# The rank scans of two query tiles cut into four parts, and the selection steps of tiles 2 and 4 spread over more heads

## What is computed

```python
idx_score = jnp.where(admissible[None], idx_score, NEG)
_, sel = lax.top_k(idx_score, topk)          # topk = 256; of equal scores the lower index wins
...
scores = jnp.einsum('bqhd,bqkd->bhqk', qb, k_sel) * scale
scores = scores - slopes[None, :, None, None] * dist[:, None]
p = jax.nn.softmax(scores, axis=-1)
```

## Time and profile before

| | |
|---|---|
| median of 3 runs | 551.23 us (550.86 to 551.24) |
| the profiled execution | 551.45 us |
| its span, first to last instruction | 549.6 us |
| PE busy | 541.5 us (99%) |
| DVE busy | 443.3 us (81%) |
| ACT busy | 371.8 us (68%) |
| POOL busy | 183.2 us (33%) |
| chain that ended last | PE 85%, DVE 11%, ACT 2%, issue 1% |
| attention loop in the span | about 311 us to the end |

### The profile page before, as it was taken

One profiled execution on the slowest core, in us unless ns is written; L12 is line 12 of the kernel. 1 busy time (PEld: TensorE's weight loads), 2 busy tenths in 40 slices (PEclk: granted clock), 3 DMA queues, 4 the chain that ended last, 5 costly groups with the idle time before them and its releaser, 6 DMA issues.

```text
span 549.6 us, 8942 instructions
## 1 busy us (share of the span) xinstructions
PE 541.5 (99%) x2968; PEld 461.8 (84%) x2968; DVE 443.3 (81%) x1111; ACT 371.8 (68%) x713; POOL 183.2 (33%) x285
## 2 busy tenths in 40 slices
PE   8999999999999999999999999999999999999997
PEld 8998888888888888887888888878888888889886
DVE  5786878899989998999978988898777888976621
ACT  5985777759996667779888567875564655565510
POOL 1871000104469996676210003573002020010230
PEclk9999999999999999999999999999999999999999
DMA  8724100004321111221222143603111202020032
GB/s 246 249 65 135 31 28 21 0 14 126 100 88 45 53 39 39 51 85 40 58 59 76 41 133 115 212 25 91 58 57 33 84 20 78 1 77 20 2 116 76
DMA packets 39982, 39.69 MB, mean 72 GB/s; under 512 B 6144, under 2 KB 28160, under 8 KB 39936
## 3 DMA queue, kind: packets, MB, share of 16 engines
q1 hardware_dynamic: 38416, 39.11, 23.7%
q10 hardware_dynamic: 1520, 0.01, 0.2%
HBM read 30.72 MB, written 8.39 MB: 71 GB/s over the span
## 4 chain that ended last, share of the span: by engine, by line
PE 85%; DVE 11%; ACT 2%; issue 1%; POOL 0%; DVEq 0%; POOLq 0%; ACTq 0%
PE ps_proj L1116 42%; PE ps_proj L1298 11%; PE ps_lg L1146 5%; PE ps_lg L1145 5%; PE ps_proj L1270 5%; PE ps_tp L1255 5%; PE ps_lg L1298 3%; DVE cand L1549 2%; PE ps_tp L1217 1%; DVE w_lo L1454 1%; PE ps_lg L1091 1%; PE ps_tp L1281 1%; DVE xT_lo L1780 1%; PE ps_tp L1133 1%; PE ps_tp L1172 1%
## 5 line engine op out<-in xcount | busy, mean ns | idle before, releaser
L1116 PE MATMUL ps_proj<-w_hi,xT_hi 128*128 128x512 f32 (+1 forms) x432 | 164.7, 381 | 0.7 <-DVE xT_lo L1409 0.5
L1116 PE MATMUL ps_proj<-w_lo,xT_hi 128*128 128x512 f32 (+1 forms) x432 | 161.2, 373 | 0.0
L1116 PE MATMUL ps_proj<-w_hi,xT_lo 128*128 128x512 f32 (+1 forms) x432 | 161.0, 373 | 0.0
L951 ACT ACTIVATE ps_lg<-score,cand 128x768 f32<-128x768 f32 (+2 forms) x96 | 96.0, 1000 | 10.6 <-DVE cand L1549 10.3
L1116 PEld LDWEIGHTS ps_proj<-w_lo,xT_hi 128*128 128x128 f32 x432 | 81.4, 188 | 15.0
L1116 PEld LDWEIGHTS ps_proj<-w_hi,xT_hi 128*128 128x128 f32 x432 | 81.4, 188 | 13.5 <-DVE xT_lo L1409 0.9
L1116 PEld LDWEIGHTS ps_proj<-w_hi,xT_lo 128*128 128x128 f32 x432 | 81.6, 189 | 11.8
L1008 ACT CAST xT_hi<-ps_tp 128x128 fp32r<-128x128 f32 (+3 forms) x89 | 40.0, 486 | 64.0 <-PE ps_tp L1255 63.9
L1780 DVE TENSOR_TENSOR xT_lo<-ps_tp,xT_hi 128x128 fp32r<-128x128 f32 (+3 forms) x89 | 47.1, 559 | 32.5 <-ACT xT_hi L1008 32.0
L992 ACT ACTIVATE lo_f<-lo_f,negmax 128x128 f32<-128x128 f32 (+7 forms) x64 | 50.2, 785 | 0.2
L1454 DVE SCALAR_TENSOR_TENSOR w_lo<-stage,g_in,w_hi 128x512 fp32r<-128x512 f32 x48 | 43.9, 918 | 7.0 <-ACT w_hi L803 6.4
(11 more groups left out here) (195 smaller groups left out, 1116.1 us busy)
## 6 DMA issues: line engine op xcount, KB each, us to landing
stage<-in_w_in_dram SPq DMA_DIRECT2D x48, 256.0 KB, 2.7
x_in<-in_x_dram SPq DMA_DIRECT2D x8, 512.0 KB, 5.1
lo_f<-in_x_dram SPq DMA_DIRECT2D x7, 512.0 KB, 4.1
out_dram<-lo_f SPq DMA_DIRECT2D x7, 512.0 KB, 3.5
q_scratch<-nat SPq DMA_DIRECT2D x8, 256.0 KB, 2.0
q_in<-q_scratch SPq DMA_DIRECT2D x8, 256.0 KB, 3.8
stage<-in_w_out_dram SPq DMA_DIRECT2D x8, 256.0 KB, 2.6
z_scratch<-nat SPq DMA_DIRECT2D x8, 256.0 KB, 2.1
```

Source lines behind the costliest of these rows:

```text
L951: act.activation(ps_lg[i % 2][:, 0:keys(t)], score[:, sc_off[t]:sc_off[t] + keys(t)], ACT.Sign, bias=cand[:, t:t + 1].bitcast(F32), scale= ...
L1116: mm = pe.matmul(ps_proj[u % 2][:, 0:n], a[:, k, rows], b[:, k, 0:n], start=(k == 0 and i == 0), stop=(k == KB - 1 and i == 2))
```

## The change

The scan of a tile is cut in parts of n // 4 for tiles 5 and 6 (192 and 224 columns, n = 768 and 896); tile 7 keeps its two halves of 512, tiles below 5 their single scan. Each part takes its start value from the last column of the part before and is a step with a `yield` of its own, so the selections of tiles 5 to 7 have four steps more. `LATE_AT` gets four heads more: head 6 of tile 2, and heads 1, 3 and 7 of tile 4.

```diff
-                cut = n // 2 if t >= SPLIT else n
+                cut = n if t < SPLIT else n // 4 if t < T - 1 else n // 2
                 then(dve.tensor_tensor_scan(rank[:, 0:cut], eq[:, 0:cut], eq[:, 0:cut], 0.0, ALU.add, ALU.max))
                 yield
-                if cut < n:
-                    then(dve.tensor_tensor_scan(rank[:, cut:n], eq[:, cut:n], eq[:, cut:n], rank[:, cut - 1:cut],
-                                                ALU.add, ALU.max))
+                for c in range(cut, n, cut):
+                    then(dve.tensor_tensor_scan(rank[:, c:c + cut], eq[:, c:c + cut], eq[:, c:c + cut],
+                                                rank[:, c - 1:c], ALU.add, ALU.max))
                     yield
...
-            LATE_AT = ((2, 4, 6, 7), (0, 1), (1, 2, 7), (1, 2, 4, 6), (0, 2, 4, 6), (0, 2, 4, 6), (0, 1, 2, 4), ())
+            LATE_AT = ((2, 4, 6, 7), (0, 1), (1, 2, 6, 7), (1, 2, 4, 6), (0, 1, 2, 3, 4, 6, 7), (0, 2, 4, 6), (0, 1, 2, 4),
+                       ())
```

## The result

| | before | after |
|---|---|---|
| median | 551.23 us (550.86 to 551.51, 7 runs) | 552.63 us (552.52 to 552.97, 7 runs) |
| profiled execution | 551.45 us | 552.57 us |
| its span | 549.6 us | 550.7 us |

The ratio is 1.0025, with a 95% interval of 1.0016 to 1.0034: the changed kernel is slower by 1.4 us. A run of both kernels beside each other on another occasion gave 552.86 against 551.44 us, again 1.0025 (1.0016 to 1.0035).

A forecast was written before the change was run, and what follows sets the result against it. PE, busy 99% of the span, was taken to bound the kernel. Terms 0.29 - 0.15 + 0.05 + 1.12 gave +1.3 us, a median of 552.5 us; range 551.0 to 553.5 us.

The forecast's parts named there:

- the turn to tile 5: PE's first transposes of tile 5, held until `lo_mix` has read both banks; the join delays them, +1.12 us.
- The price of a part: Scan parts with a start value on DVE: 0.63 us for 192 columns, 0.70 for 224, from 2.03 ns a column.
- Tile 4, head 7, +1.12: Join of 896 columns in a formerly empty head delays `lo_mix`, on which PE waits: +1.12 us, bounds +0.8 and +1.3.
- The rival with slack at this turn: First transposes of tile 5 held by PE's own work, join free, smaller steps gain: -1.3, 549.9 us, chance 0.10.
- Tile 4, heads 0 to 6, -0.15 and +0.05: Head 2's shorter step cuts the wait before the query transposes, -0.15 us; head 3's step sticks out before `lo_q`, +0.05.
- Tile 2, +0.29: Steps of 0.67 us in heads 6 and 7 replace "le" of 1.05, all ahead of `lo_mix`: +0.29 us.
- the rival with POOL: Tile 2, head 6: new scan waits for the end of POOL's L752, adding 0.98 us: +2.3, 553.5 us, chance 0.15.
- These waits: PE's waits: 0.47 us before tile 1's first output block, 0.32 before tile 4's query transposes; called the most recoverable there.
- the sign that was to show tile 2: PE's wait for `lo_mix` ahead of tile 1's first output block grown to about 0.75 us, not gone.

The follow-up runs named there:

- the best version: Changed kernel with other heads: tile 2 in 1, 2, 4, 7; tile 3 in 1, 2, 4, 5, 6; tile 4 without 7: 550.66 us.

## Why the prediction was right, point by point

The forecast was +1.3 us, measured +1.4 and +1.42; A to Z moved by +1.29 us. Of its terms the largest, the turn to tile 5, was right by its mechanism; that of tile 2 came out by luck.

**The price of a part**: right. 0.63 and 0.70 us were forecast for 192 and 224 columns with a start value. The undisturbed ones took 0.61 and 0.68. Line L1608 of the changed kernel, minimum, median and maximum; the maximum is the part beside POOL:

```profile
L1608 DVE TENSOR_TENSOR_SCAN rank<-eq,rank x7: 614/678/1393, 353.9 to 460.3; 128x192 f16<-128x192 int8 x3, 128x224 f16<-128x224 int8 x3, 128x512 f16<-128x512 int8 x1
```

**Tile 4, head 7, +1.12**: right, in size and mechanism. The step took 1.12 us, C to D grew by 1.20, PE starts 0.83 us behind `lo_mix` as forecast, and two edits from opposite sides show it: 1.1 us given back by taking the instruction away, 0.96 us lost by moving it alone. PE's wait is 1.20 us where near 1.3 was forecast. The rival with slack at this turn is refuted by the second.

**Tile 4, heads 0 to 6, -0.15 and +0.05**: right. In head 0 DVE did stand idle for ACT's high part (0.28 us), so the earlier end was worth nothing. The wait ahead of the query transposes fell to 0.17, since `lo_pT` is held by ACT: 405.62 + 0.69 = 406.31 is when it starts. B to C is 0.20 shorter, and of the 1.20 in C to D, some 0.07 lie at the transposes behind `lo_q`, where head 3's part sticks out: `lo_q` came 0.71 us behind ACT's `hi_q` before (408.65 for 407.94), which would be 408.59 now (407.88 + 0.71), and it starts at 408.66:

```profile
398.13 0.68 DVE L1600 TENSOR_SCALAR eq<-score,cand 128x896 int8<-128x896 f32 x1
398.85 0.15 DVE L1601 TENSOR_SCALAR room<-cnt 128x1 f32<-128x1 f32 x1
399.27 0.89 DVE L1781 TENSOR_TENSOR xT_lo<-ps_tp,xT_hi 128x512 fp32r<-128x512 f32 x2 [0.28 <-ACT xT_hi L1008]
...
405.26 0.68 DVE L1608 TENSOR_TENSOR_SCAN rank<-eq,rank 128x224 f16<-128x224 int8 x1
406.31 0.89 DVE L1781 TENSOR_TENSOR xT_lo<-ps_tp,xT_hi 128x512 fp32r<-128x512 f32 x2 [0.38 <-ACT xT_hi L1008]
407.12 0.81 DVE L1771 CUSTOM_DVE_ANT_0 lo_f<-ps_lg,score 128x640 f32<-128x640 f32 x1
...
407.86 0.68 DVE L1608 TENSOR_TENSOR_SCAN rank<-eq,rank 128x224 f16<-128x224 int8 x1
408.66 1.53 DVE L1671 SCALAR_TENSOR_TENSOR xT_hi<-ps_tp,gq,xT_hi 64x512 fp32r<-64x512 f32 x2
```

**Tile 2, +0.29**: the sum was right (+0.29 on DVE, +0.32 in A to B), but three of its steps were wrong, and the first two cancelled.
- "In heads 1 and 2 DVE gets about half a microsecond back each time, but nobody waits for it there ... worth nothing." POOL waited. Its scalings of weights stand beside those scans, and each shorter scan let POOL go on sooner: 1.33 us became 0.93 and 0.99, 0.74 us less in sum. POOL's L738 and L752 came 0.91 us earlier, which is 0.72 us counted from mark A, and the pair of `lo_w` became 0.74 us shorter. The same holds in the other kernels: L761 takes 1.33 or 1.34 us twice and the pair 2.38 to 2.42 wherever tile 5 is in halves; with parts in heads 1 and 2 it is 0.93 and 0.99 or 1.00, and the pair 1.64 to 1.67, or 1.90 with a part in head 4, where L738 starts 0.26 us later. POOL, tile 2 of the changed kernel:

```profile
351.63 0.93 POOL L761 TENSOR_SCALAR hi_f<-hi_f,g_out 128x512 f32<-128x512 f32 x1
...
353.93 0.99 POOL L761 TENSOR_SCALAR hi_f<-hi_f,g_out 128x512 f32<-128x512 f32 x1
...
356.28 0.69 POOL L761 TENSOR_SCALAR hi_f<-hi_f,g_out 128x512 f32<-128x512 f32 x1
```

- The part in head 6 was priced at 0.67 and took 1.43 us. That was the rival with POOL, and its mechanism is real: with a count that reads one operand in its place, 0.75 us are gone. Its sum of +2.3 wasn't reached, because the earlier POOL gives 0.74 back in the same stretch. The forecast had named that as the argument against, but as a way to escape the collision and not as a gain beside it. By the Trainium skill, SBUF — State Buffer, section "Who interferes with whom", whoever issues first blocks the other. The trace agrees: L752 starts at 365.30, the scan at 365.67, and it is the scan that is stretched. In tile 2 of the kernel before it was the other way round: the scan in head 1 started at 351.59, POOL's L761 at 351.80, and L761 took 1.33 us.
- "These waits are the whole of what smaller steps can give back there": PE had a third wait, for the third `lo_w` (0.45 us at the weight load, some 0.3 us of PE's time), and POOL's earlier work took it away. So the sign that was to show tile 2, a wait for `lo_mix` grown to about 0.75, failed: it grew to 1.06, since PE was there 0.28 us sooner.

That the gain of 0.74 and the extra loss of 0.76 on DVE cancel is chance, and with it that the term came out. Moving that step to head 4 drops the loss and keeps 0.48 of the 0.74 on DVE and the whole 0.3 of the third wait. A to B is then 0.78 us shorter than before in the best version, nearly all of what that version has over the kernel before: 0.47 for `lo_mix` and 0.3 for `lo_w`.

## What to carry to other kernels

Where the work of one engine is laid out by hand between the calls of others, price a moved step by what stands right behind it and who waits for that, not by its length: the same instruction cost nothing in head 6 and 1 us in head 7. Cutting work into smaller parts pays where the part's length was what somebody waited for; here that was 0.15 us in tile 4, and 0.3 us in tile 2 by way of POOL and the third `lo_w`. And when an instruction gets shorter in a place where the engine that sets the pace doesn't wait, look whether an instruction of another engine was stretched beside it, since that one may get ahead and meet other work later on. A sum that comes out is no proof of its steps: look for the wait that the forecast named, and for waits at weight loads, which the matmuls' own rows need not name.

## What was not expected of the hardware

- A scan part of 0.61 us took 1.39 beside a POOL instruction with two operands in SBUF, while a count with one operand took 0.62 us at the same place beside the same instruction. The stretch ran from POOL's side as well: POOL's L761, 0.69 us undisturbed, took 1.33 us beside scans of 384 columns and 0.93 and 0.99 beside parts of 192.
- The stretched scan ended 0.41 us behind POOL's L752 (367.06 for 366.65), less than the 0.61 us that such a scan takes by itself, so part of its time passed beside L752. In head 4 it was the same: 360.84 against 360.44 for POOL's L763, 0.40 us.
- Mark A, which stands ahead of every edited step, comes at between 346.96 and 347.59 us in eleven kernels and one repeat that take the same steps up to there. The changed kernel had 347.10 and 347.03 in two profiled executions. Differences of medians under 0.3 us were therefore read by stretches here; what moves mark A stays open.
